# Layer normalisations: gate product left in PSUM for the residual sum, and a tile's factors made ahead of the scaling of the preceding tile

## The reference

```python
m = silu(c) @ w_mod[l] + b_mod[l]          # shift, scale, gate for each sub-layer
h = x * (1 + scale) + shift
x = layer_norm(ALPHA * x + gate * f(h), ln_g, ln_b)
def layer_norm(x, g, b, eps=1e-5):
    mu = x.mean(-1); var = square(x - mu).mean(-1)
    return (x - mu) * rsqrt(var + eps) * g + b
```

## Time and profile before

| | |
|---|---|
| three runs | 5467.97, 5468.78, 5473.68 us |
| the profiled execution's own time | 5471.31 us |
| its span in the profile | 5469.6 us |
| PE, matmul | 5148.1 us busy, 94% of the span |
| DVE | 2765.6 us, 51% |
| ACT | 1416.1 us, 26% |
| POOL | 1494.2 us, 27% |
| granted TensorE clock, mean | 0.96 of full speed |

### The profile page before, as it was taken

How to read it: one execution, slowest core, us unless ns; L and a number is a source line. 1 busy time by engine, 2 the same in 40 slices (tenths; PEclk the granted TensorE clock), 3 DMA queues, 4 the chain that set the end, 5 groups by cost and what they waited for, 6 DMA issues and landing times.

```text
span 5469.6 us, 70249 instructions
## 1 busy us (share of the span) xinstructions
PE 5148.1 (94%) x30167; PEld 4571.9 (84%) x30167; DVE 2765.6 (51%) x4785; ACT 1416.1 (26%) x1532; POOL 1494.2 (27%) x839
## 2 busy tenths in 40 slices
PE   6999779999999989999899999899999999999998
PEld 3767679999999978888666678889999999878886
DVE  2162669914444146666555541389524442166666
ACT  0110022223444222222222222112234443222222
POOL 0020222332222265542011110123322222455531
PEclk7969999999999999999799999999999999999999
DMA  7141022334444478886210011113334444588873
GB/s 293 63 165 59 20 77 82 121 118 153 156 158 154 167 255 300 304 302 258 84 38 33 31 44 46 46 60 112 119 135 155 157 155 153 195 312 302 294 295 142
DMA packets 295263, 835.85 MB, mean 153 GB/s; under 512 B 23923, under 2 KB 157299, under 8 KB 242727
## 3 DMA queue, kind: packets, MB, share of 16 engines
q1 hardware_dynamic: 91680, 520.91, 25.8%
q10 hardware_dynamic: 158216, 176.07, 9.4%
q0 software_dynamic: 45056, 134.38, 7.2%
HBM read 674.40 MB, written 156.80 MB: 152 GB/s over the span
## 4 chain that ended last, share of the span: by engine, by line
PE 89%; DVE 6%; POOL 2%; DMA 1%; ACT 1%; issue 1%; SPq 0%; DVEq 0%; ACTq 0%; POOLq 0%
PE PS L584 20%; PE PS L586 20%; PE PS L585 20%; PE PS L635 4%; PE PS L716 3%; PE PS L429 3%; PE PS L829 3%; PE PS L807 3%; PE PS L489 3%; PE PS L791 2%; POOL A L1847 1%; PE PS L576 1%; DVE EP L1348 1%; DMA ring<-in_w_mod 1%; PE PS L713 1%
## 5 line engine op out<-in xcount | busy, mean ns | idle before, releaser
L584 PE MATMUL PS<-hH,wH 128*128 128x320 f32 x4608 | 1439.2, 312 | 29.5 <-DVE hL L1116 28.4
L585 PE MATMUL PS<-hL,wH 128*128 128x320 f32 x4608 | 1425.0, 309 | 0.0
L586 PE MATMUL PS<-hH,wL 128*128 128x320 f32 x4608 | 1425.0, 309 | 0.0
L1836 POOL TENSOR_TENSOR wL<-raw,wH 128x2048 fp32r<-128x2048 f32 x144 | 669.1, 4647 | 1659.4 <-ACT wH L1570 1659.4
L584 PEld LDWEIGHTS PS<-hH,wH 128*128 128x128 f32 x4608 | 867.0, 188 | 30.7 <-issue 29.2
L585 PEld LDWEIGHTS PS<-hL,wH 128*128 128x128 f32 x4608 | 867.2, 188 | 0.0
L586 PEld LDWEIGHTS PS<-hH,wL 128*128 128x128 f32 x4608 | 866.2, 188 | 0.0
L1570 ACT ACTIVATE wH<-raw 128x2048 fp32r<-128x2048 f32 x272 | 520.5, 1914 | 1111.4 <-PE PS L586 1052.0
L586 PE MATMUL PS<-wH,WL 128*128 128x512 f32 x2048 | 803.8, 392 | 0.0
L1223 DVE TENSOR_TENSOR wL<-raw,wH 128x2048 fp32r<-128x2048 f32 x128 | 293.4, 2292 | 463.3 <-ACT wH L1570 463.3
L1855 POOL DMA_INDIRECT ubuf<-in_v,idxV x256 | 356.3, 1392 | 582.3 <-DVE acc L1235 539.6
(11 more groups left out here) (331 smaller groups left out, 6571.9 us busy)
## 6 DMA issues: line engine op xcount, KB each, us to landing
raw<-in_u SPq DMA_DIRECT2D x128, 1024.0 KB, 4.8
raw<-in_v SPq DMA_DIRECT2D x128, 1024.0 KB, 4.9
expert_acts<-abuf ACTq DMA_DIRECT2D x128, 640.0 KB, 2.9
expert_gates<-wide ACTq DMA_DIRECT2D x64, 1024.0 KB, 5.1
wide<-expert_acts SPq DMA_DIRECT2D x64, 1024.0 KB, 5.6
ring<-in_w_mod SPq DMA_DIRECT2D x48, 1024.0 KB, 8.7
wide<-expert_gates SPq DMA_DIRECT2D x16, 2048.0 KB, 11.8
gb<-expert_gates SPq DMA_DIRECT2D x16, 2048.0 KB, 12.0
```

Of the source, the lines that this page charges most:

```text
L584: nc.tensor.matmul(out, lhsH, rhsH, start=start, stop=False)
L585: nc.tensor.matmul(out, lhsH, rhsL, start=False, stop=False)
L586: return nc.tensor.matmul(out, lhsL, rhsH, start=False, stop=stop)
L1836: G.tensor_tensor(wL[:, n % NSPLIT, :], raw[:, n % NRAW, :], wH[:, n % NSPLIT, :].bitcast(f32), ALU.subtract).then_inc(lo_u, 1)
```

## The change

Three edits, all on VectorE; the other engines' programs stay as they are.

The product of result and gate row is written back to where the result lay (PSUM, and `acc0` for the prompt tile of n = 1 and 3) and no longer to `f`. The residual sum reads it there. The semaphore that tells PE that the banks have been read (`out_evac`, `v_evac`, `oo_evac`) is raised by the residual sum and no longer by the product.

The wait for `dev_ready`, the reciprocal and `nmr` of tile i stand directly behind `bn_aggr` of tile i, ahead of the multiplication by `ln_g` of tile i-1.

```diff
+    t0_added = sem("t0_added")
...
+                halves = lambda z: z.rearrange("p (c d) -> p c d", c=2)
                 for i in range(NT + 1):
                     if i < NT:
-                        gated(i)
-                        link(V.scalar_tensor_tensor(x[:, i, :], x[:, i, :], ALPHA, f[:, i, :], ALU.mult, ALU.add))
+                        part, evac, count = gated(i)
+                        V.scalar_tensor_tensor(halves(x[:, i, :]), halves(x[:, i, :]), ALPHA, part, ALU.mult, ALU.add).then_inc(evac, 1)
+                        ve.wait_ge(evac, count)
                         for c in range(2):
                             do(V.bn_stats(stat[:, 2 * i + c, :], x[:, i, c * 512:(c + 1) * 512]))
                         settle()
                         V.bn_aggr(mv[:, i, :], stat[:, 2 * i:2 * i + 2, :]).then_inc(ln_stats, 1)
+                        ve.wait_ge(dev_ready, 2 + n * NT + i + 1)
+                        link(V.reciprocal(rstd[:, i:i + 1], rstd[:, i:i + 1]))
+                        V.scalar_tensor_tensor(nmr[:, i:i + 1], mv[:, i, 0:1], -1.0, rstd[:, i:i + 1], ALU.mult, ALU.mult).then_inc(ln_factors, 1)
                     t = i - 1
                     if t >= 0:
                         ve.wait_ge(ln_normed, n * NT + t + 1)
...
                             V.tensor_tensor(x[:, t, :], x[:, t, :], rows[1], ALU.add).then_inc(x_ready, 1)
-                    if i < NT:
-                        ve.wait_ge(dev_ready, 2 + n * NT + i + 1)
-                        link(V.reciprocal(rstd[:, i:i + 1], rstd[:, i:i + 1]))
-                        V.scalar_tensor_tensor(nmr[:, i:i + 1], mv[:, i, 0:1], -1.0, rstd[:, i:i + 1], ALU.mult, ALU.mult).then_inc(ln_factors, 1)
...
                 def gated(t):
                     ve.wait_ge(products, at["eo", t])
-                    V.tensor_tensor(f[:, t, :].rearrange("p (c d) -> p c d", c=2), PS[:, 2 * (t % 4):2 * (t % 4) + 2, :],
-                                    rowsB[:, 2 + (t > 0), :].rearrange("p (c d) -> p c d", c=2), ALU.mult).then_inc(out_evac, 1)
-                    ve.wait_ge(out_evac, t + 1)
+                    part = PS[:, 2 * (t % 4):2 * (t % 4) + 2, :]
+                    link(V.tensor_tensor(part, part, rowsB[:, 2 + (t > 0), :].rearrange("p (c d) -> p c d", c=2), ALU.mult))
+                    return part, out_evac, t + 1
...
                 def gated(t):
                     if t == 0:
-                        link(V.tensor_tensor(f[:, 0, :], acc0[:], rowsP[2], ALU.mult))
-                    else:
-                        ve.wait_ge(products, at["vt", l, t - 1])
-                        V.tensor_tensor(f[:, t, :].rearrange("p (c d) -> p c d", c=2), PS[:, 2 * t - 2:2 * t, :],
-                                        rowsP[3].rearrange("p (c d) -> p c d", c=2), ALU.mult).then_inc(v_evac, 1)
-                        ve.wait_ge(v_evac, l * 4 + t)
+                        link(V.tensor_tensor(acc0[:], acc0[:], rowsP[2], ALU.mult))
+                        return acc0[:].rearrange("p (c d) -> p c d", c=2), t0_added, l + 1
+                    ve.wait_ge(products, at["vt", l, t - 1])
+                    part = PS[:, 2 * t - 2:2 * t, :]
+                    link(V.tensor_tensor(part, part, rowsP[3].rearrange("p (c d) -> p c d", c=2), ALU.mult))
+                    return part, v_evac, l * 4 + t
```

More of the change, by code:

```diff
@@ L1378, in gated @@
                     ve.wait_ge(products, at["oo", t])
-                    V.scalar_tensor_tensor(f[:, t, :].rearrange("p (c d) -> p c d", c=2), PS[:, 2 * (t % 4):2 * (t % 4) + 2, :], ssq[:, t:t + 1],
-                                           rowsO[:, 2 + (t > 0), :].rearrange("p (c d) -> p c d", c=2), ALU.mult, ALU.mult).then_inc(oo_evac, 1)
-                    ve.wait_ge(oo_evac, t + 1)
+                    part = PS[:, 2 * (t % 4):2 * (t % 4) + 2, :]
+                    link(V.scalar_tensor_tensor(part, part, ssq[:, t:t + 1], rowsO[:, 2 + (t > 0), :].rearrange("p (c d) -> p c d", c=2),
+                                                ALU.mult, ALU.mult))
+                    return part, oo_evac, t + 1
                 layer_norm(2, [rowsO[:, 0, :], rowsO[:, 1, :]], gated)
```

## The result

The changed kernel took 5450.97 us (median of 8 runs, 5443.68 to 5459.33) against 5468.38 us (8 runs, 5460.59 to 5474.82) for the kernel before on the same chip: ratio 0.997, 95% interval 0.9959 to 0.9981. On another chip, beside two later versions, it took 5449.17 us against 5465.64, ratio 0.9971, interval 0.996 to 0.9981. So the change saves some 17 us (10 to 22), 0.3%. The forecast was 5454.5 us, in the range.

What follows compares the result with a forecast made beforehand. PE ends 89% of the chain, but VectorE's time per tile sets the ends of n = 1 and n = 3. -5.86 - 7.1 - 0.70 - 0.70 = -14.3 takes 5471.31 to 5457.0; runs' median 2.5 lower: 5454.5 us, range 5449 to 5463.

Steps and rivals of the forecast that it cites:

- The step: Per tile in n = 1 and n = 3, product to next product: 5.79 us instead of 7.48.
- The wait that comes in its stead: Tile 4 of each normalisation: GpSimd's addition holds L903(4), which ends at T+4.77 instead of T+4.86, T being nmr(4)'s start.
- the joins: Ends of the four normalisations, where following work waits for VectorE: savings carry over, 5.86 us after n = 1, 0.70 after n = 0, 2.
- The PSUM operands: Product and residual sum in all normalisations: product into PSUM costs +0.02 us, sum with one PSUM input 0.
- the outputs' term in n = 3: End of n = 3: ScalarE's queue reaches the outputs 2.2 us earlier after nmr(4), -1.2 us taken, -1.5 to 0 possible.
- the slower rival: Experts' starts: shifted idle time leaves PE's clock slow for 30 us, costing 14 us and cancelling the gain; chance 0.03.
- the sum, -14.3: Whole kernel: -5.86 (n = 1), -7.1 (n = 3) and -0.70 each (n = 0, n = 2).
- (a): Tile 4: L903(4) is not held, only L910 waits for GpSimd's addition; 5450 us, chance 0.06.
- (b): n = 1 and n = 3: operations with PSUM and SBUF inputs are held too, the sum by 2.2 us; 5467.7, chance 0.05.
- (c): After n = 1: loads or a phase of the experts' stage take its saving back; 5460.4 us, chance 0.10.
- (d): All normalisations: nmr's 2.33 us are its own, not GpSimd's; step 7.96 us, +9 us, 5478, chance 0.03.

Runs made afterwards that it cites:

- PSUM alone: Changed kernel with wait, reciprocal and nmr moved back behind the multiplication by ln_g, product still in PSUM: 5464.95 us beside 5463.85 for the kernel before.
- order alone: Kernel before with wait, reciprocal and nmr moved ahead of L903, product still written to f: 5455.15 us beside 5463.85 for the kernel before.

## Why the prediction was right, and where it was wrong

**Right.** nmr was held by GpSimd's addition: without additions it takes 0.16 us at its old place, and a later release frees it too. The order cures that, and PSUM keeps the sum from taking nmr's place: PSUM alone is worth 0.3 us of the tail stretch, order alone 8.1, both 15.1. The step was forecast at 5.79 us and is 5.81. The wait that comes in its stead, L903(4) behind GpSimd's addition, was forecast with L910's end 6.03 us after nmr(4); it is 6.06. Predicted and measured agree to 0.1 us in n = 0, 1 and 2, and the joins carry over. In n = 0 and n = 2 VectorE's L1108 (now L1110), ahead of the experts, starts 1.26 us after the start of L910 (now L916) in both profiles, and PE's first product of the odd mixer (L690, now L691) begins in both profiles after the same 2.96 us of idle time, ended by VectorE's L882 (now L883).

**The PSUM operands.** Product 1.23 and sum 1.220 us, from SBUF 1.224: the sum is not dearer from PSUM. The product costs 0.01 to 0.02 us more, as taken. The 0.065 us for each sum that I took from the Trainium skill, "VectorE: DVE Perf Modes", section on the TRN2 errata, does not show at this size; the measurement decides.

**Wrong: the outputs' term in n = 3**, -1.2 us of the -7.1. The data did end 8.4 us after nmr(4), as I had worked out (8.2). But the step took for granted that the end of the span follows the last transfer, because it did so before, when the DRAIN of GpSimd's program happened to end at the same moment. The DRAIN moves with GpSimd's last addition, which starts 1.4 us later against nmr(4) than it did (1.38 us behind it, before 0.03 ahead). It ends 7.95 us behind that addition, so the stretch behind L910/L916 grew by 1.3 us where I had 1.2 less, and n = 3 gave 4.5 us; moving that one addition to VectorE brought the span's end from 11.9 to 8.5 us after nmr(4).

**Left out: the clock.** The tail stretch fell by 3.4 us more than the four normalisations. By stages, from the end of one normalisation to the first nmr of the next, the experts of layer 0 gave 1.3 us, the odd mixer 2.4, and the experts of layer 1 took 0.3 more. Most of it shows at two places, both at a restart of PE after idle time. After a pause in the value products of layer 0, PE stands at half clock (granted 0.50, the 1.2 GHz level) for 6 us in the kernel before and for 3 in the changed one, by windows of 3 us from its restart (columns: window, its length, busy us of PE, PEld, DVE, ACT and POOL with counts, granted clock, DMA share, GB/s), first before, then after:

```profile
1990.70:1993.70 3.00, 3.00 (x8) 2.33 (x8) 2.90 (x3) 0.00 (x0) 2.10 (x3) 0.50 0.91 287
```

```profile
1986.10:1989.10 3.00, 3.00 (x14) 2.44 (x14) 2.90 (x3) 0.00 (x0) 2.10 (x3) 1.00 0.92 272
```

The same work, 1.3 us sooner. And in the odd mixer, 32 to 38 us after its first product, the clock is 0.68 before and 0.91 after:

```profile
2700.00:2706.00 6.00, 6.00 (x16) 3.25 (x16) 0.00 (x0) 0.00 (x0) 0.00 (x0) 0.68 0.08 31
```

```profile
2688.10:2694.10 6.00, 6.00 (x19) 3.37 (x19) 0.00 (x0) 0.00 (x0) 0.00 (x0) 0.91 0.07 27
```

By its end PE is 1.4 us further on than before. The other 1.0 us of the odd mixer is the sum of gains and losses of up to 1.5 us at later places, which fall otherwise in each profile; PSUM alone, slower than the changed kernel by 1.5 us in this stage, had 0.9 us of it too. The first place showed the same in both profiles of the changed kernel and in order alone; PSUM alone, whose nmr is held as before, was like the kernel before. Whether the clock owes that to the shift of the restarts, or to what PE did ahead of them, no run here settles. I had put the clock at 1 to 2 us in the range, and beside the slower rival at 14; it went the other way, by little. So the sum, -14.3 against the tail stretch's -15.1, is near partly by luck: two errors, +2.6 and -3.4, offset one another. (The terms as written add up to -14.36, and the chances to 0.98; neither alters the forecast.)

**The medians** say -17 (10 to 22) where the tail stretch says -15. That lies within the interval, and the stretch ahead varies by 9 us between executions, so the 2 us between them are not resolved.

**The rivals.** (a), L903(4) not held: no, 3.33 us. (b), operations with a PSUM input held: no, 1.22 to 1.23 us beside the addition. Its price was also wrong, by the factor two: I charged the sum 2.2 us, but the addition starts 0.17 us after the product, and a held sum loses 1.1 to 1.2 us, as order alone shows. (c), a join that doesn't carry over: no. (d), nmr's time its own: no, by two experiments.

## What to carry to other kernels

A tiny VectorE operation of 2.3 us is a wait in disguise: look for a GpSimd instruction that ends with it, and ask of each VectorE operation beside GpSimd whether both its inputs lie in SBUF: here those were held and the ones with an input in PSUM were not. Moving the victim is half a cure; what then runs beside GpSimd must have an input in PSUM. Releasing the GpSimd work behind the victim, with the product in PSUM and the last tile's addition taken off GpSimd, was worth 8 us of the tail stretch more; what each of these gives by itself, no run separates. At the end of a program look at what closes each engine, not at the last transfer: here 7.95 us pass behind GpSimd's last instruction, so in a kernel like this one the last piece of work should not be its own.

## What the runs showed of the hardware that I had not expected

GpSimd's program closes with a DRAIN that ends 7.95 us after its last instruction: 10.3 us behind an addition of 2.34, 8.05 behind a memset of 0.10. In the kernel without additions, where the last GpSimd instruction is an indirect transfer, it lay 70 us before the end and cost nothing.

A held operation loses a little less than the hold. L909(4) comes up 0.10 us after GpSimd has started; it takes 3.33 us and ends 1.09 us after GpSimd, where alone it takes 1.22.
